# A fused GLA / SSD / Conformer / DeltaNet backbone with MoE on one core: the conformer tiles of the last input projection come one period earlier, and one modulation step comes one group of weights earlier

## The chip, the cores and the metric

One core of a Trainium2 chip runs the whole two-layer model as one program. The metric is the device time of one execution in microseconds, lower is better. The kernel before took 2444.59 us, the median of three runs (2441.27 to 2473.6).

## The reference, cut to what matters

The second layer's mixer (`mixer_cd`) starts with one large input projection and cuts its result into eight kinds of columns:

```python
def cd_stream(h, w_in, b_in, gdn_conv_w, gdn_a_log, gdn_dt_bias):
    bsz, t, _ = h.shape
    ga, gb, q, k, v, og, a_raw, b_raw = split_cols(h @ w_in + b_in, CD_SPLITS)
    glu = ga * jax.nn.sigmoid(gb)
    qkv = jax.nn.silu(dwconv(jnp.concatenate([q, k, v], axis=-1), gdn_conv_w)).astype(F32)
    q, k, v = split_cols(qkv, (GDN_QK, GDN_QK, GDN_V))
    ...
    q = l2norm(heads(q)) * GDN_DK ** -0.5
    k = l2norm(heads(k))

def conformer_conv(u, rows, dw_w, dw_b, ln_g, ln_b):
    bsz, t, ch = u.shape
    y = dwconv(u.reshape(bsz * rows, t // rows, ch), dw_w, dw_b).reshape(bsz, t, ch)
    return jax.nn.silu(layernorm(y, ln_g, ln_b))
```

`glu` has 1024 channels, 8 tiles of 128; its depthwise convolution `conformer_conv` is 31 wide. `q`, `k` and `v` have 8 tiles each too and pass a depthwise convolution that is 3 wide. Context tokens (256) and latent tokens (256) lie side by side, T = 512 columns; the conformer, `q` and the output gate `og` are wanted for the 256 latent tokens alone. The delta-rule scan (`gdn_scan`) follows.

## The kernel before, in words

Activations lie with channels on the 128 partitions and the 512 tokens along the free axis, float32 throughout. The weights stream from HBM through a ring of three slots of 4 MB (`Ring`, `weight_groups`): a group of eight 128-column weight tiles of the projection fills a slot, and so does each half of a modulation step (a slice of the conditioning matmul, loaded by four DMAs of 1 MB). SyncE issues all these loads in the order of `weight_groups`; the load of group n waits until TensorE has used group n - 3, which is counted by the semaphore `w_used`.

The place of the change is the projection of the second layer, `project(PLAN["cd"], ...)`. The list `CD_ALL` names its 49 tiles in the order in which they are computed: first `small` (gates), then eight periods of six tiles: `gb`, `ga`, `k`, `v`, `og`, `q` of one channel chunk. Each engine walks the same list with a loop over j, each in its own program order, and they meet at semaphores:

- TensorE (L489) multiplies tile j: 16 records in the trace for eight k-steps, 512 columns wide for `small`, `k` and `v` (called wide below) and 256 for the others (narrow). It may run four tiles ahead of their copy out of PSUM (`proj_evacuated`). Two tiles behind (`lag=2`), after the matmuls of tile j, it transposes the finished `k`, `v` or `q` tile j - 2 (L504) once `turn_ready` says that it is there.
- ScalarE copies tile j out of PSUM (L1191 for the tiles with a convolution, L1198 for `gb` with a sigmoid and for `ga`, L1208 for `og`). After tile j it finishes the convolution of tile j - 1 with a Silu (L1176), for which it waits for `conv_done`; and it squares the transposed `k` or `q` tile j - 4 for the l2 norm (`kq_squares`, L1169, into `mrow` as scratch).
- VectorE does at step j, in this order: the product `ga * sigmoid(gb)` into `gluR` (L1629) if tile j is a `ga`; the 3-wide convolution (L1650, L1652, L1654) if tile j is `k`, `v` or `q`; the copy of the transposed tile j - 2 (L1658); then some of the 31 taps of the conformer convolution (`conformer_taps`, L1618 for the first, L1620 for the others) by the table `glu_at`; then the steps of `gate_softplus` that are fixed to numbers j (L1675 and L1677 at j = 2, `softplus_head` at j = 8, and so on).

`CONF_STEPS` cuts the 31 taps of a chunk into five portions (7, 6, 6, 6, 6), given out at the step of its `ga` tile and the four after it. So before the change each portion stands alone in its step, and the last one stands in step 48, the last tile's.

Between the tiles come two modulation steps. `CD_MODS = {3: 1, 4: 2}` puts step 1 ahead of the group of tiles number 3 (j = 24) and step 2 ahead of group 4 (j = 32): TensorE multiplies it (L416), ScalarE copies it into `mrow` (L1124), TensorE transposes it from there (L432) one tile later. The same table sets the order of the weight stream in `weight_groups`.

After the tiles `gdn_gates` transposes the gates (L641, L642) as soon as the last `q` tile has been copied; ScalarE takes the root of the squares (L1249) once its last `kq_squares` is done; then the scan starts.

Of the kernel before, what the change touches and what calls it, by code (L numbers as in the profile page):

```python
# [43 lines left out]
AB_GLA = [("small", 0)] + [("q", i) for i in range(4)] + [("k", i) for i in range(4)] \  # L44
    + [("v", i) for i in range(8)] + [("r", i) for i in range(8)]
AB_SSD = [("xs", i) for i in range(8)] + [("bm", 0), ("bm", 1), ("cm", 0), ("cm", 1)] + [("z", i) for i in range(8)]
CD_ALL = [("small", 0)] + [(k, i) for i in range(8) for k in ("gb", "ga", "k", "v", "og", "q")]
CONF_STEPS = [(0, 7), (7, 13), (13, 19), (19, 25), (25, 31)]


CD_MODS = {3: 1, 4: 2}


def weight_groups():


    def mod(layer, r):
        return [(f"mod{layer}{r}", i, 4) for i in range(2)]
# [9 lines left out]
    for i in range(7):  # L68
        if i in CD_MODS:
            g += mod(1, CD_MODS[i])  # L70
        g += [("cd", 8 * i, 1)]
# [25 lines left out]
def hybrid_backbone(nc, A, out):  # L97
    rg = Ring()
    with ExitStack() as ctx:
# [3 lines left out]
        def sb(name, shape, dt=F32, stack=ctx):  # L103
            return stack.enter_context(nc.sbuf_tensor(name, shape, dt))
# [20 lines left out]
        small = sb("small", [P, T])  # L125
# [81 lines left out]
        with ExitStack() as st:  # L207
            gluR = sb("gluR", [P, KD, ROWS, PADW], F32, st)
            og = sb("og", [P, KD, SEQ], F32, st)
# [107 lines left out]
        def plan(stage, tiles, kinds, bias, bias0):  # L317


            made = []  # L320
            for j, (kind, i) in enumerate(tiles):
                how, turn, both = kinds[kind]
                made.append(dict(group=rg.at[stage, j - j % 8], place=j % 8, kind=kind, i=i, how=how,
                                 no=counts["tile"], last=j % 8 == 7 or j == len(tiles) - 1,
                                 turn=counts["turn"] if turn else None, conv=counts["conv"] if how == "conv" else None,
                                 c0=0 if both else SEQ, bias=col(bias, bias0 + j)))
                counts["tile"] += 1
                counts["turn"] += turn
                counts["conv"] += how == "conv"
            return made  # L330

        PLAN = {"gla": plan("gla", AB_GLA, GLA_KINDS, "ab_b", 0), "ssd": plan("ssd", AB_SSD, SSD_KINDS, "ab_b", len(AB_GLA)),
                "cd": plan("cd", CD_ALL, CD_KINDS, "cd_b", 0)}

# [63 lines left out]
        def _(pe):  # L398
# [5 lines left out]
            def modulation_rows(layer, r):  # L404

                first = rg.first[f"mod{layer}{r}"]
                if layer == 0 and r == 0:
                    pe.wait_ge(sg("cond_ready"), 1)
                else:
                    pe.wait_ge(sg("mod_row_copied"), 3 * layer + r)  # L410
                for kh in range(2):
                    group_in(first + kh)
                    w = slot(first + kh).rearrange("p g (k n) -> p g k n", k=4)
                    for k in range(4):
                        for g in range(4):
                            last = mm(ps[6][32 * g:32 * g + 32, :], act_c[:, 4 * kh + k, :], w[:, g, k, :],  # L416
                                      start=(kh == 0 and k == 0), stop=(kh == 1 and k == 3),
                                      tile_position=(0, 32 * g))
                    last.then_inc(w_used, 1)
                pe.drain().then_inc(sg("mod_rows"), 1)  # L420

            def modulation_turn(layer, r):

                pe.wait_ge(sg("mod_row_copied"), 3 * layer + r + 1)
                if layer == 0 and r == 0:
                    pe.wait_ge(sg("norm_ms"), 1)
                else:
                    pe.wait_ge(sg("mod_added"), 3 * layer + r)
                    if r == 0:
                        pe.wait_ge(sg("norm_ms"), 2)  # L430
                for q in range(4):
                    nc.tensor.transpose(ps[7][:, q * P:(q + 1) * P], mrow[:, q * P:(q + 1) * P], ident[:, :])  # L432
                pe.drain().then_inc(sg("mod_turned"), 1)
# [5 lines left out]
            def modulation_between(j):  # L439

                if j % 8 == 0 and j // 8 in CD_MODS:
                    modulation_rows(1, CD_MODS[j // 8])
                if j % 8 == 1 and j // 8 in CD_MODS:
                    modulation_turn(1, CD_MODS[j // 8])

# [1120 lines left out]
        def _(dve):  # L1566
# [46 lines left out]
            def project(made, dest, taps=None, gates=False, between=None):  # L1613
                def conformer_taps(i, lo, hi):
                    y = conf[:, i, :].rearrange("p (r c) -> p r c", r=ROWS)
                    for w in range(lo, hi):
                        if w == 0:
                            V.tensor_scalar(y, gluR[:, i, :, 0:GW], col("conf_w", i), col("conf_b", i), ALU.mult, ALU.add)  # L1618
                        else:
                            V.scalar_tensor_tensor(y, gluR[:, i, :, w:w + GW], col("conf_w", 8 * w + i), y, ALU.mult, ALU.add)  # L1620
                        dve.drain()

                glu_at = {j + n: (p["i"], lo, hi) for j, p in enumerate(made) if p["how"] == "glu" for n, (lo, hi) in enumerate(CONF_STEPS)}
                for j in range(len(made) + 2):
                    if j < len(made) and made[j]["how"] == "glu":

                        i = made[j]["i"]
                        dve.wait_ge(sg("glu_in"), i + 1)
                        V.tensor_tensor(gluR[:, i, :, CK // 2:CK // 2 + GW], gsig[i % 2].rearrange("p (r c) -> p r c", r=ROWS),  # L1629
                                        gval[i % 2].rearrange("p (r c) -> p r c", r=ROWS), ALU.mult)  # L1630
                        dve.drain().then_inc(sg("glu_done"), 1)
                    if j < len(made) and made[j]["how"] == "conv":

                        p = made[j]
                        c, s0 = p["conv"], p["c0"] // SEQ
                        if p["kind"] == "k" and p["i"] == 0 and p["group"] >= rg.first["cd"]:
                            dve.wait_ge(sg("conv_silu"), c)
                            dve.drain()
                            V.memset(cpad2[:, :, :, 0:1], 0.0)
                            V.memset(cpad2[:, :, :, SEQ + 1:SEQ + 2], 0.0)  # L1640
                            dve.drain().then_inc(sg("conv_pads"), 1)
                        dve.wait_ge(sg("conv_in"), c + 1)
                        if c >= 2:
                            dve.wait_ge(sg("conv_silu"), c - 1)
                            before = conv_turn[c - 2]
                            if before is not None:
                                dve.wait_ge(sg("turn_done"), before + 1)
                        to = conv_sum(p)[:, p["c0"]:T].rearrange("p (s t) -> p s t", t=SEQ)
                        w, pad = taps(p), conv_pad(p)
                        V.tensor_scalar(to, pad[:, s0:2, 1:SEQ + 1], w[1], None, ALU.mult)  # L1650
                        dve.drain()
                        V.scalar_tensor_tensor(to, pad[:, s0:2, 0:SEQ], w[0], to, ALU.mult, ALU.add)  # L1652
                        dve.drain()
                        V.scalar_tensor_tensor(to, pad[:, s0:2, 2:SEQ + 2], w[2], to, ALU.mult, ALU.add).then_inc(sg("conv_done"), 1)  # L1654
                    if j >= 2 and made[j - 2]["turn"] is not None:
                        p = made[j - 2]
                        dve.wait_ge(sg("turn_done"), p["turn"] + 1)
                        V.tensor_copy(dest(p), ps[4 + p["turn"] % 2][:, p["c0"]:T].rearrange("p (t c) -> p t c", c=P)).then_inc(sg("turn_copied"), 1)  # L1658
                    if gates and 1 <= j < 24 and j % 3 == 1:
                        gla_magnitude(j // 3)  # L1660
                    if gates and j >= 3 and j % 3 == 0:
                        gla_sums(j // 3 - 1)
                    if j in glu_at:
                        conformer_taps(*glu_at[j])
                    if between is not None:
                        between(j)

# [777 lines left out]
def pack_columns(np, a):  # L2445
# [37 lines left out]
    at0 = COL_AT["cd_b"]  # L2483
    tiles(b, CD_ALL, CD_PLACE)
    for dst, src, n in CD_SMALL:
# [45 lines left out]
def lay_out(np, a):  # L2531
    w2p = np.zeros((P, 8, P), np.float32)
    for d in range(2):
# [6 lines left out]
        "ab_wo": pack_out(np, a["ab_w_out"][0]),  # L2540
        "cd_w": pack_projection(np, a["cd_w_in"][0], CD_ALL, CD_PLACE, CD_SMALL),
        "cd_wo": pack_out(np, a["cd_w_out"][0]),
# [22 lines left out]
```

## Time and profile before

| | |
|---|---|
| median of three runs | 2444.59 us (2441.27 to 2473.6) |
| profiled execution | 2442.07 us, of which its span 2440.3 us |
| TensorE matmul busy | 1991.5 us, 82% |
| VectorE busy | 781.5 us, 32% |
| ScalarE busy | 498.4 us, 20% |
| GpSimd busy | 192.2 us, 8% |
| granted TensorE clock, mean | 0.924 of full speed |
| read from HBM | 524.26 MB, 215 GB/s over the span |

The span is the time from the first to the last instruction of the profiled execution; the execution's own time has 1.8 us more around it. The projection that the change touches runs from 1328 us to 1612 us of the span. In it VectorE is much busier than its 32% over the whole span.

### The profile page before, as it was taken

How to read it: one execution, taken by the hardware profiler on the slowest of the kernel's cores; microseconds unless marked ns; L12 is line 12 of the kernel's file. 1: busy time of each engine (PE TensorE's matmuls, PEld its weight loads, DVE VectorE, ACT ScalarE, POOL GpSimd, SP SyncE). 2: the span in 40 equal slices, each digit the busy share in tenths (PEclk: the TensorE clock that was granted, in tenths of full speed). 3: DMA queues.
4: the chain of work that ended last, by engine and by line, in shares of the span. 5: the costliest groups of instructions: out<-in, count | busy, mean ns of one | idle time of the engine just before them, and what ended most of it. 6: DMA issues, size and time to landing. Idle time of an engine off the chain costs nothing.

```text
span 2440.3 us, 30684 instructions
## 1 busy us (share of the span) xinstructions
PE 1991.5 (82%) x12598; PEld 1040.8 (43%) x12598; DVE 781.5 (32%) x1456; ACT 498.4 (20%) x1037; POOL 192.2 (8%) x230
## 2 busy tenths in 40 slices
PE   5998869987699698898887998979998866666665
PEld 2443744434444333333323655657777622212112
DVE  1112643347710300000002874757765210000001
ACT  2333312222200201000003422344443100000001
POOL 0000000032100000000002100025541000000000
PEclk9999989998999899999999999989998977788887
DMA  9013012250001599999997146110001369999996
GB/s 371 31 69 127 11 58 92 90 208 1 1 35 69 216 416 431 429 433 429 429 430 302 70 157 265 70 70 2 2 2 70 139 274 430 430 431 433 430 431 256
DMA packets 57519, 527.15 MB, mean 216 GB/s; under 512 B 2864, under 2 KB 4144, under 8 KB 43056
## 3 DMA queue, kind: packets, MB, share of 16 engines
q1 hardware_dynamic: 55776, 522.55, 51.5%
q10 hardware_dynamic: 1616, 2.76, 0.3%
q8 instruction: 97, 1.59, 0.3%
q14 instruction: 30, 0.25, 0.0%
HBM read 524.26 MB, written 1.05 MB: 215 GB/s over the span
## 4 chain that ended last, share of the span: by engine, by line
PE 50%; DMA 31%; DVE 9%; issue 3%; ACT 3%; DVEq 1%; PEld 1%; SPq 1%; PEldq 1%; ACTq 0%; POOL 0%
DMA ring<-in_moe_w 28%; PE bank L489 20%; PE bank L988 9%; PE bank L916 5%; PE bank L882 2%; DVE ring L1763 2%; PE bank L594 2%; PE bank L663 1%; PE bank L686 1%; DMA ring<-in_cd_w 1%; DMA router<-in_router 1%; DVE x L2187 1%; DMA ring<-in_ab_w 1%; SPq L296 1%; PEld bank L489 1%
## 5 line engine op out<-in xcount | busy, mean ns | idle before, releaser
L489 PE MATMUL bank<-hT,ring 128*128 128x512 f32 (+1 forms) x1504 | 556.8, 528 | 23.5 <-DMA ring<-in_cd_w 11.2
L988 PE MATMUL bank<-ring,xgs 128*32 128x512 f32 x3072 | 397.0, 672 | 142.7 <-DMA ring<-in_moe_w 141.3
L489 PEld LDWEIGHTS bank<-hT,ring 128*128 128x128 f32 x1504 | 287.4, 194 | 273.2 <-issue 241.6
L988 PEld LDWEIGHTS bank<-ring,xgs 128*32 128x32 f32 x3072 | 111.2, 121 | 401.8 <-issue 309.4
L988 PE MATMUL bank<-ring,hT 128*32 128x512 f32 x1536 | 201.6, 680 | 85.3 <-DMA ring<-in_moe_w 85.3
L2009 DVE SCALAR_TENSOR_TENSOR x<-bank,modT,x 128x256 f32<-128x256 f32 x96 | 42.4, 481 | 480.6 <-PE bank L1014 480.6
L988 PEld LDWEIGHTS bank<-ring,hT 128*32 128x32 f32 x1536 | 56.6, 122 | 217.7 <-issue 165.0
L1998 DVE TENSOR_TENSOR hT<-sils,bank 128x512 f32<-128x512 f32 x24 | 15.8, 686 | 368.5 <-PE bank L988 368.5
L1620 DVE SCALAR_TENSOR_TENSOR x<-gluR,cols,x 128x256 f32<-128x256 f32 x240 | 116.1, 484 | 16.0 <-issue 0.4
L1403 ACT ACTIVATE sils<-bank 128x512 f32<-128x512 f32 x24 | 13.5, 595 | 417.9 <-PE bank L988 417.9
L916 PE MATMUL bank<-mixA,ring 128*128 128x512 f32 x128 | 58.5, 612 | 7.7 <-DVEq L2146 7.7
L594 PE MATMUL bank<-xs_t,x 128*128 (+1 forms) x256 | 38.9, 311 | 28.9 <-DVE x L2124 28.9
L977 PEld LDWEIGHTS bank<-pick,htok 128*128 128x128 f32 x384 | 47.7, 203 | 22.2 <-issue 17.2
L2383 POOL TENSOR_TENSOR ring<-ring,pmask 128x512 f32<-128x512 f32 x40 | 50.9, 1271 | 77.2 <-DVE ring L1751 66.6
L1393 ACT ACTIVATE xgs<-bank 128x512 f32<-128x512 f32 x24 | 14.3, 597 | 206.8 <-PE bank L977 206.8
L916 PE MATMUL bank<-zmix,ring 128*128 128x512 f32 x128 | 56.2, 592 | 0.0
L2367 POOL MEMSET gluR<- 128x3008 f32 x1 | 2.6, 2609 | 679.5 <-DVEq L2019 679.5
L977 PE MATMUL bank<-pick,htok 128*128 128x128 f32 x384 | 52.0, 293 | 4.7 <-DVEq L1980 4.7
L416 PE MATMUL bank<-ring,act_c 128*32 128x512 f32 x384 | 45.6, 628 | 7.8 <-DMA ring<-in_mod_w 6.0
L1419 ACT ACTIVATE pgate<-bank 128x512 f32<-128x512 f32 x24 | 13.5, 595 | 187.4 <-PE bank L988 187.4
L594 PEld LDWEIGHTS bank<-xs_t,x 128*128 128x128 f32 x256 | 35.3, 217 | 38.3 <-issue 29.6
L1014 PE MATMUL bank<-gateT,pgate 128*128 128x256 f32 x192 | 50.6, 394 | 0.3
(451 smaller groups left out, 2385.2 us busy)
## 6 DMA issues: line engine op xcount, KB each, us to landing
ring<-in_moe_w SPq DMA_DIRECT2D x96, 4096.0 KB, 22.4
ring<-in_mod_w SPq DMA_DIRECT2D x48, 1024.0 KB, 11.7
ring<-in_cd_w SPq DMA_DIRECT2D x6, 4096.0 KB, 21.1
ring<-in_ab_w SPq DMA_DIRECT2D x5, 4096.0 KB, 21.7
ring<-in_ab_wo SPq DMA_DIRECT2D x2, 4096.0 KB, 15.5
ring<-in_cd_wo SPq DMA_DIRECT2D x2, 4096.0 KB, 13.6
x<-in_xT SPq DMA_DIRECT2D x1, 2048.0 KB, 10.4
ring<-in_ab_w SPq DMA_DIRECT2D x1, 2048.0 KB, 15.7
```

Of the source, the lines that this page charges most:

```text
L416: last = mm(ps[6][32 * g:32 * g + 32, :], act_c[:, 4 * kh + k, :], w[:, g, k, :], start=(kh == 0 and k == 0), stop=(kh == 1 and k == 3), t ...
L489: last = mm(ps[p["no"] % 4][:, p["c0"]:T], w[:, k, :], hT[:, k, p["c0"]:T], start=(k == 0), stop=(k == KD - 1))
L594: last = mm(ps[2 + hp][:, P * t:P * t + P], mat[hp][:, t * P:(t + 1) * P], tile(t), start=True, stop=True, skip_group_check=True)
L882: last = mm(ps[c % 4][:, SEQ:T], w[:, k, :], conf[:, k, :] if k < 8 else og[:, k - 8, :], start=(k == 0), stop=(k == 15))
L916: last = mm(ps[c % 4][:, c0:T], w[:, k, :], mixed(k), start=(k == 0), stop=(k == 15))
L977: last = mm(ps[(4, 7)[b % 2]][:, k * P:(k + 1) * P], htok[:, 2 * s + tt, ch:ch + P], pick[:, s, tt, P * q:P * q + P], start=(tt == 0), sto ...
L988: last = mm(ps[banks + s][32 * j:32 * j + 32, :], lhs[s][:, 4 * kh + k, 32 * j:32 * j + 32], w[:, j, k, :], start=(kh == 0 and k == 0), st ...
L1014: last = mm(ps[(4, 7)[dt % 2]][:, 256 * s:256 * s + 256], yex[s][:, dt * P:(dt + 1) * P], gateT[:, s, q, :], start=True, stop=True, skip_g ...
L1620: V.scalar_tensor_tensor(y, gluR[:, i, :, w:w + GW], col("conf_w", 8 * w + i), y, ALU.mult, ALU.add)
L1763: last = V.copy_predicated(to[r, :, :, :], mask[r, 0, :].unsqueeze(1).unsqueeze(1).broadcast_to([64, 2, NT, 64]), S)
L2009: last = V.scalar_tensor_tensor(x[:, dt, cc], ps[(4, 7)[dt % 2]][:, cc], mod(layer, 5, dt, s), x[:, dt, cc], ALU.mult, ALU.add)
L2383: G.tensor_tensor(Hb[(l + 1) % 3], Fb[p % 2], pmask[:, l - 1, :].unsqueeze(1).unsqueeze(1).broadcast_to([P, 2, NT, 64]), ALU.mult).then_in ...
```

## The change

`CD_ALL` is written in another order: the `gb` and `ga` tiles of chunk i + 1 stand ahead of the `k`, `v`, `og`, `q` tiles of chunk i. So the list begins `small`, `gb` 0, `ga` 0, `gb` 1, `ga` 1, `k` 0, ..., and the last period has `k`, `v`, `og`, `q` of chunk 7 alone. Since two `ga` tiles now stand two steps apart at the start, `glu_at` holds a list for each step, and two portions of taps can stand in one step. `CD_MODS` puts modulation step 1 ahead of tile group 2 (j = 16) instead of group 3. No tile, tap or byte is added or removed. In the kernel after, the lines behind the edits stand 2 or 6 lines further down.

```diff
-CD_ALL = [("small", 0)] + [(k, i) for i in range(8) for k in ("gb", "ga", "k", "v", "og", "q")]
+CD_ALL = [("small", 0), ("gb", 0), ("ga", 0)]
+for _i in range(8):
+    CD_ALL += [(k, _i + 1) for k in ("gb", "ga") if _i < 7] + [(k, _i) for k in ("k", "v", "og", "q")]
...
-CD_MODS = {3: 1, 4: 2}
+CD_MODS = {2: 1, 4: 2}
...
-                glu_at = {j + n: (p["i"], lo, hi) for j, p in enumerate(made) if p["how"] == "glu" for n, (lo, hi) in enumerate(CONF_STEPS)}
+                glu_at = {}
+                for j, p in enumerate(made):
+                    if p["how"] == "glu":
+                        for n, (lo, hi) in enumerate(CONF_STEPS):
+                            glu_at.setdefault(j + n, []).append((p["i"], lo, hi))
...
-                    if j in glu_at:
-                        conformer_taps(*glu_at[j])
+                    for steps in glu_at.get(j, []):
+                        conformer_taps(*steps)
```

VectorE at the start of the projection, before: the product of chunk 0, seven taps, two gate operations, two memsets, the convolution of `k` 0 (into `wk`), six taps, the convolution of `v` 0, six taps, the copy of the transposed `k` 0.

```order
447 L1629 TENSOR_TENSOR gluR<-rstd,rst64 128x4x64
448 L1618 TENSOR_SCALAR x<-gluR,cols 128x256
449 L1620 SCALAR_TENSOR_TENSOR x<-gluR,cols,x 128x256 x6
450 L1675 TENSOR_SCALAR k_t<-small,cols 64x512
451 L1677 SCALAR_TENSOR_TENSOR v_t<-k_t 64x512
...
457 L1620 SCALAR_TENSOR_TENSOR x<-gluR,cols,x 128x256 x6
458 L1650 TENSOR_SCALAR wk<-wk,cols 128x512
459 L1652 SCALAR_TENSOR_TENSOR wk<-wk,cols 128x512
460 L1654 SCALAR_TENSOR_TENSOR wk<-wk,cols 128x512
461 L1620 SCALAR_TENSOR_TENSOR x<-gluR,cols,x 128x256 x6
462 L1658 COPY k_t<-bank4 128x512
```

The same place after the change.

```order
452 L1622 SCALAR_TENSOR_TENSOR x<-gluR,cols,x 128x256 x6
453 L1635 TENSOR_TENSOR gluR<-rstd,rst64 128x4x64
454 L1622 SCALAR_TENSOR_TENSOR x<-gluR,cols,x 128x256 x6
455 L1620 TENSOR_SCALAR x<-gluR,cols 128x256
456 L1622 SCALAR_TENSOR_TENSOR x<-gluR,cols,x 128x256 x6
...
462 L1622 SCALAR_TENSOR_TENSOR x<-gluR,cols,x 128x256 x12
463 L1656 TENSOR_SCALAR wk<-wk,cols 128x512
464 L1658 SCALAR_TENSOR_TENSOR wk<-wk,cols 128x512
465 L1660 SCALAR_TENSOR_TENSOR wk<-wk,cols 128x512
466 L1622 SCALAR_TENSOR_TENSOR x<-gluR,cols,x 128x256 x12
467 L1664 COPY k_t<-bank4 128x512
```

Between the product of chunk 0 and the copy of `k` 0 there stand now a second product and 50 taps instead of 19. The steps 4 to 6 hold two portions each, and 26 taps (7, 6, 6 and 7) stand ahead of the first convolution instead of 7.

VectorE at the end of the projection, before: the last convolutions (`v` 7, then `q` 7) and copies, each with six taps behind it. The last row is the first of `gdn_gates`.

```order
605 L1650 TENSOR_SCALAR wk<-wk,cols 128x512
606 L1652 SCALAR_TENSOR_TENSOR wk<-wk,cols 128x512
607 L1654 SCALAR_TENSOR_TENSOR wk<-wk,cols 128x512
608 L1620 SCALAR_TENSOR_TENSOR x<-gluR,cols,x 128x256 x6
609 L1658 COPY k_t<-bank5 128x512
610 L1620 SCALAR_TENSOR_TENSOR x<-gluR,cols,x 128x256 x6
611 L1650 TENSOR_SCALAR wk<-wk,cols 128x256
...
614 L1658 COPY v_t<-bank4 128x512
615 L1620 SCALAR_TENSOR_TENSOR x<-gluR,cols,x 128x256 x6
616 L1658 COPY q_t<-bank5 128x256
617 L1700 TENSOR_SCALAR rkq<-rkq 128x48
```

The same place after the change.

```order
605 L1656 TENSOR_SCALAR wk<-wk,cols 128x512
606 L1658 SCALAR_TENSOR_TENSOR wk<-wk,cols 128x512
607 L1660 SCALAR_TENSOR_TENSOR wk<-wk,cols 128x512
608 L1664 COPY q_t<-bank4 128x256
609 L1664 COPY k_t<-bank5 128x512
610 L1656 TENSOR_SCALAR wk<-wk,cols 128x256
611 L1658 SCALAR_TENSOR_TENSOR wk<-wk,cols 128x256
612 L1660 SCALAR_TENSOR_TENSOR wk<-wk,cols 128x256
613 L1664 COPY v_t<-bank4 128x512
614 L1664 COPY q_t<-bank5 128x256
615 L1706 TENSOR_SCALAR rkq<-rkq 128x48
```

The taps are gone from the last steps; the last portion stands four steps earlier.

## Rows read from the trace of the kernel before

**Rows 1.** The page's chain of waits, shares of the span by engine.

```profile
PE 50%; DMA 31%; DVE 9%; issue 3%; ACT 3%; DVEq 1%; PEld 1%; SPq 1%; PEldq 1%; ACTq 0%; POOL 0%
```

**Rows 2.** Waits of PE, 1320 to 1620 us: total us, times, longest.

```profile
PE bank L489 <- DMA ring<-in_cd_w: 11.2, 2, 6.1
...
PE bank L504 <- ACTq L1178: 4.0, 3, 3.6
PE bank L641 <- DVE q_t L1658: 3.2, 1, 3.2
```

**Rows 3.** Groups by line, 1328 to 1614 us.

```profile
L1620 DVE SCALAR_TENSOR_TENSOR x<-gluR,cols,x 128x256 f32<-128x256 f32 x240 | 116.1, 484 | 16.0 <-issue 0.4
```

**Rows 4.** Timeline of PE: start us, us, line, operation, count.

```profile
1328.16 33.69 PE L489 MATMUL bank<-hT,ring 128*128 128x512 f32 x96 [6.88 <-ACT hT L1144]
...
1366.02 3.62 PE L489 MATMUL bank<-hT,ring 128*128 128x256 f32 x16
1369.90 3.69 PE L489 MATMUL bank<-hT,ring 128*128 128x256 f32 x16 [0.26 <-issue]
...
1402.29 7.03 PE L489 MATMUL bank<-hT,ring 128*128 128x512 f32 x16
...
1450.04 7.07 PE L416 MATMUL bank<-ring,act_c 128*32 128x512 f32 x64
1462.22 5.72 PE L489 MATMUL bank<-hT,ring 128*128 128x256 f32 x16 [5.11 <-DMA ring<-in_cd_w]
...
1515.07 6.59 PE L489 MATMUL bank<-hT,ring 128*128 128x256 f32 x16 [6.06 <-DMA ring<-in_cd_w]
...
1606.45 0.69 PE L504 MATMUL bank<-ident,wk 128*128 128x128 f32 x2 [3.58 <-ACTq L1178]
1610.34 1.09 PE L641 MATMUL bank<-ident,small 128*128 128x128 f32 x4 [3.20 <-DVE q_t L1658]
```

**Rows 5.** Timeline of DVE, the first steps of the projection.

```profile
1345.32 0.45 DVE L1629 TENSOR_TENSOR gluR<-rstd,rst 128x256 f32<-128x256 f32 x1 [13.65 <-ACTq L1201]
1345.89 0.44 DVE L1618 TENSOR_SCALAR x<-gluR,cols 128x256 f32<-128x256 f32 x1
...
1349.82 0.48 DVE L1675 TENSOR_SCALAR k_t<-small,cols 64x512 f32<-64x512 f32 x1
...
1351.19 0.06 DVE L1639 MEMSET wk<- 128x4 f32 x1
...
1359.20 0.49 DVE L1650 TENSOR_SCALAR wk<-wk,cols 128x512 f32<-128x512 f32 x1 [1.53 <-ACTq L1193]
...
1361.26 3.28 DVE L1620 SCALAR_TENSOR_TENSOR x<-gluR,cols,x 128x256 f32<-128x256 f32 x6
1364.60 0.69 DVE L1658 COPY k_t<-bank 128x512 f32<-128x512 f32 x1
1365.21 3.28 DVE L1620 SCALAR_TENSOR_TENSOR x<-gluR,cols,x 128x256 f32<-128x256 f32 x6
```

**Rows 6.** Timeline of DVE, the last steps of the projection.

```profile
1604.44 0.35 DVE L1650 TENSOR_SCALAR wk<-wk,cols 128x256 f32<-128x256 f32 x1 [0.17 <-issue]
...
1606.43 3.27 DVE L1620 SCALAR_TENSOR_TENSOR x<-gluR,cols,x 128x256 f32<-128x256 f32 x6
1609.77 0.42 DVE L1658 COPY q_t<-bank 128x256 f32<-128x256 f32 x1
```

**Rows 7.** Timeline of ACT, the last steps of the projection.

```profile
1602.02 0.47 ACT L1191 ACTIVATE wk<-bank,cols 128x256 f32<-128x256 f32 x1 [3.35 <-PE bank L489]
1605.94 0.42 ACT L1176 ACTIVATE wk<-wk 128x256 f32<-128x256 f32 x1 [3.45 <-DVE wk L1654]
1606.53 0.31 ACT L1169 ACTIVATE mrow<-k_t 128x128 f32<-128x128 f32 x1 [0.17 <-DVE v_t L1658]
...
1611.06 1.28 ACT L1249 ACT_TABLE_LOAD   x1
```

**Rows 8.** Timeline of SP, the load that the first wait is for.

```profile
1449.29 0.37 SPq L302 DMA_DIRECT2D ring<-in_cd_w  x1
```

**Rows 9.** Stretches: PE busy (x), then other engines, PEclk, DMA share, GB/s.

```profile
1462.20:1468.00 5.80, 5.78 (x19) 4.75 (x20) 0.00 (x0) 0.02 (x1) 0.00 (x0) 0.65 1.05 388
...
1606.00:1610.00 4.00, 0.69 (x2) 0.29 (x2) 3.55 (x8) 1.64 (x9) 0.00 (x0) 0.53 0.85 352
```

## The prediction

> **What bounds the kernel now.** I read the page's chain first: over the whole span TensorE holds half of it and the waits for weights almost a third [rows 1]. The change touches neither the experts nor any byte, so only the projection's 284 us matter. There TensorE's own waits come next [rows 2]: 11.2 us in two waits for projection weights, 4.0 us for ScalarE ahead of transposes (3.6 of it once) and 3.2 us for VectorE ahead of the gates. All else is TensorE at work: the tiles follow each other without a gap, a narrow one every 3.5 us and a wide one every 6.9 us [rows 4]. So the stage is bound by TensorE, with the two loads after the modulation steps and the tail as the holes.
>
> The tail's hole has VectorE in it. It holds 240 taps of 0.484 us, 116.1 us in all, in this stage [rows 3]. At the end ScalarE has copied `q` 7 out of PSUM at 1602.49, but the convolution begins only at 1604.44, behind six taps; its transposed tile is copied at 1609.77, behind six taps more that began at 1606.43 [rows 6, 7]. TensorE idles 3.58 and 3.20 us there [rows 4]. These taps leave the tail, and that is what the change gives. What it takes is at the other end, where VectorE gets two chunks' taps at once.
>
> **What goes: the tail.** I replay ScalarE's path to its root table load, which stood at 1611.06 [rows 7]. TensorE's last matmul ends at the same time if nothing else moved. Copy at 1602.02, done 1602.49; VectorE is free and starts the convolution some 0.15 later, at 1602.65. From its first operation to the Silu it took 1.50 us (1604.44 to 1605.94), so Silu at 1604.15, done by 1604.57. The transposes began 0.51 after the Silu's start, so at 1604.66; with 0.69 for them the copy starts at about 1605.4, and is visible to ScalarE 0.45 later, at 1605.85. But ScalarE has a task there that was hidden before: the four squares of `k` 7 (0.3 us each), which ran at 1606.53 while VectorE was busy with taps. They now run from 1604.6 to 1605.9, just beside the transposes and the copy. Then come the squares of `q` 7, and the table load at about 1606.8: from the copy's start to the load it was 1.29 us (1609.77 to 1611.06), of which the last 0.8 are these squares. Gain: 1611.06 - 1606.8 = 4.2 us. If the `k` squares fell wholly behind the copy it would be 3 us, and if the clock in the gates' matmuls (0.53 of full speed in 1606 to 1610 [rows 9]) stays up as well, 5 us. I take 4.2.
>
> **What comes: the start.** VectorE's prices are [rows 5]: product 0.57 (1345.32 to 1345.89), first portion of seven taps 3.93 (1345.89 to 1349.82), gate operations 1.37 (1349.82 to 1351.19), wide convolution 2.06 (1359.20 to 1361.26), six taps 3.34 (1361.26 to 1364.60), copy 0.61 (1364.60 to 1365.21); a narrow convolution 1.4 [rows 6]. Walking the new order from the same 1345.32: taps end 1349.8, gates 1351.2, six taps 1354.5, product of chunk 1 1355.1, six taps 1358.45, seven taps 1362.4, the two memsets and `k` 0's convolution 1364.6, two portions 1371.3, `v` 0's convolution 1373.35, two portions 1380.0, copy of `k` 0 1380.6, a portion 1384.0, `q` 0's convolution 1385.4.
>
> TensorE, from the same start: its first group of 96 records ends with `og` 0 at 1361.85 [rows 4]; with two narrow tiles more ahead of it that is 1368.8. Transposes of `k` 0 (0.45), then `q` 0 to 1372.7. Now it wants `v` 0, whose Silu and hand-over follow the convolution by 0.75: 1374.1, a wait of 1.4. Transposes, two narrow tiles, 1381.5. Now it wants `q` 0: 1385.4 plus 0.05 to the Silu and 0.51 from it to the transposes, 1386.0, a wait of 4.5. Together 5.9 us where before there was none. A backlog cannot be larger than the second chunk's work (0.57 + 3.93 + 4 x 3.34 = 17.9) less the 6.9 us of the two tiles that moved ahead and less VectorE's idle time in those steps, 1.53 us of it in the rows shown: 9.5 us. From below it is nothing, if the tiles in front of ScalarE's copies give more room than I count. I take 5.9.
>
> After that VectorE is not late again: a period holds 0.57 + 3.93 + 4 x 3.34 + 2 x 2.06 + 1.4 + 3 x 0.5, some 25 us, against TensorE's 2 x 6.9 + 4 x 3.5 + 1, some 29. The rest of the backlog goes in the first weight wait, and this one comes some 40 us earlier, at j = 16; by the same replay VectorE has nothing to do for 9 us there.
>
> **The clock.** A stop of TensorE costs more than itself. After the idle 5.11 us ahead of 1462.22 the narrow tile took 5.72 instead of 3.6, with 0.65 of full speed granted in 1462.2 to 1468.0; after 6.06 us one took 6.59 [rows 4, 9]. These are stretches at 1.2 GHz between ones at 2.4. The new stop of 4.5 us is the nearest to the first, which cost 2.1 us; nothing shows that 4.5 is enough, so the bounds are 0 and 3.0. I take 2.0.
>
> The Trainium skill ("TensorE: Matmul & The Clock Gate", section "Why this matters for your kernels") speaks against this change: an idle gap between bursts of matmuls sends the engine back to its lower clock. The trace agrees at the two weight waits. By the page's "What's actually happening" the point of switching varies from run to run; the sum would then be 4.0 with the loss and 2.0 without it.
>
> **The two weight waits and the modulation step.** Each wait is for the group of projection weights behind a modulation step. Its load can go out only when the group before it has been used (1449.29 [rows 8]), lands 12.9 us later, and 7.07 us of modulation rows lie beside it [rows 4]. In the stream of the changed kernel the two halves of step 1 stand between tile groups 1 and 2; with three slots the load of group 2 takes the slot of group 1, so it goes out when the tiles of group 1 are done, just ahead of the modulation rows, and the wait is as long as before. The number of DMAs and their bytes are the same; SyncE issues a modulation half in place of tile group 2 before the stage begins, and its rows are wanted only after 16 tiles. Behind the first awaited load now stands another projection load instead of four modulation ones, as behind the second before. That one's wait and first tile together were 12.65 against 10.83; about 0.5 of the difference is that no transposes lie inside that wait, the rest a first tile at a lower clock. Now the places are swapped, so I take +0.3 for both waits together, bounds 0 and 1.1. Moving step 1 costs nothing else: its DVE and ACT parts (two short operations) go where the old ones stood in the period. Left at j = 24 it would copy its row into `mrow` just where ScalarE squares `q` 2 into it, so the order needs the new place.
>
> **Sum.** +5.9 + 2.0 - 4.2 + 0.3 = +4.0 us. On the profiled execution's own 2442.07 that is 2446.1; the median of the runs, 2444.59, lies 2.5 above that execution, and gives 2448.6. I predict 2447. A measurement of this kernel can tell about 2% from no change, 49 us, and nothing in the stage is that large: all TensorE waits in it are 25 us.
>
> **Rivals.**
> - The start's stop is absorbed. If the two stops only eat into the first weight wait, 4.2 us are left as gain: 2438 on the profiled execution. For it: the wait follows 25 us later, and VectorE's backlog does end there. Against: the load goes out when TensorE has used the tiles before it, so it moves with TensorE [rows 8]. Only a load already on its way could absorb anything. Chance 0.15, 2438 to 2443.
> - The backlog spreads. The place is the second period: the portions of chunk 1 and `softplus_head` stand one behind the other ahead of `k` 1 and `v` 1. If each of VectorE's steps is 5% dearer than in my rows (GpSimd is at its masks until 1357), 50 us of backlog make 2.5 us more at `q` 0, and `v` 1 and `q` 1 are late by 1 to 3 us each too, with a second drop of the clock (2 to 3 us). Price: 4.0 + 2.5 + 3 + 2.5 = +12, 2454 on the profiled execution; it decides from where VectorE reaches `q` 0 after about 1388. For it: my replay leaves only tenths between VectorE and TensorE at `v` 1. Against: the period's slack of 4 us. Chance 0.2, 2450 to 2458.
> - The tail's gain isn't real, since ScalarE's table loads or squares set it: +7 instead of +4, 2449. Chance 0.1.
>
> **How the numbers follow.** My forecast, slightly slower and not to be told from no change, has 0.55. The four cases lie between 2438 and 2458, which is the range; it leaves out a median lifted by executions like the one of 2473.6. Faster by over 2%: 0.01. Slower by over 2%: 0.01, for such a draw. Within: 0.98.
>
> **What would show it.** In the timeline of the changed kernel, PE should idle about 1.4 us ahead of the transposes of `v` 0 and 4.5 us ahead of those of `q` 0, near 1373 and 1382 us, released by ScalarE's hand-over, with VectorE's taps without a gap before it. The granted clock there tells the second term: the tiles behind, `k` 1 and `v` 1, take 6.9 us each if it stays up. The waits for projection weights should be two again, near 1420 and 1515, of 5 to 6 us each. The two waits at the tail should fall from 3.58 and 3.20 to about 2 and 0.5, and the root's table load should come 5 us after ScalarE's last copy out of PSUM instead of 9. Wrong would be: a weight wait shortened by the stop before it (first rival), stops at `v` 1 or `q` 1 of over 1 us (second), or a table load that still follows 8 us or more behind the copy (third).

## The result and the profile after

The changed kernel is slightly slower: 2443.86 us (median of 20 runs, 2440.54 to 2449.1) against 2441.15 us for the kernel before in 20 runs. The ratio is 1.0016, with a 95% interval of 1.0009 to 1.0023; that is 3.9 us of 2441 (2.2 to 5.6), well within 2%. The two medians differ by 2.7 us. The prediction was 2447 us, and +4.0 us by its sum.

The span of the profiled execution is 2439.7 us against 2440.3, which looks like a gain and is none: in that execution TensorE reached the projection 5.2 us earlier, through stages that the change does not touch. So I compare a stretch, here and below: from TensorE's first projection matmul to the table load for the root of the squares, the last thing that the change moves. Before it was 1611.06 - 1328.16 = 282.9 us [rows 4, 7]; after it is 1610.19 - 1322.95 = 287.2 us, 4.3 more. What follows that table load is the same, 829.2 us before and 829.5 after. In the profiled executions below it lies between 829.1 and 829.7, except 828.2 in tail_out, while the start of the stretch lies anywhere from 1323 to 1331 us.

TensorE's timeline after, the rows that answer to [rows 4]. Columns are start us, duration us, engine, line and operation; in brackets the idle time ahead and what ended it (a q behind an engine's name, as in ACTq, stands for that engine's sequencer):

```profile
1322.95 40.49 PE L491 MATMUL bank<-hT,ring 128*128 128x512 f32 x128 [6.88 <-ACT hT L1146]
...
1369.75 0.66 PE L506 MATMUL bank<-ident,wk 128*128 128x128 f32 x4 [1.96 <-ACTq L1180]
1370.25 7.07 PE L491 MATMUL bank<-hT,ring 128*128 128x256 f32 x32
1381.68 0.44 PE L506 MATMUL bank<-ident,wk 128*128 128x128 f32 x2 [4.36 <-ACTq L1180]
1381.96 19.05 PE L491 MATMUL bank<-hT,ring 128*128 128x512 f32 x48
...
1421.82 6.14 PE L491 MATMUL bank<-hT,ring 128*128 128x256 f32 x16 [5.69 <-DMA ring<-in_cd_w]
...
1518.17 5.76 PE L491 MATMUL bank<-hT,ring 128*128 128x256 f32 x16 [6.35 <-DMA ring<-in_cd_w]
...
1532.53 0.44 PE L506 MATMUL bank<-ident,wk 128*128 128x128 f32 x2 [0.48 <-ACTq L1180]
1532.81 17.35 PE L491 MATMUL bank<-hT,ring 128*128 128x512 f32 x48
...
1607.98 0.44 PE L506 MATMUL bank<-ident,wk 128*128 128x128 f32 x2 [1.70 <-ACTq L1180]
1609.02 0.63 PE L643 MATMUL bank<-ident,small 128*128 128x128 f32 x4 [0.61 <-DVE q_t L1664]
```

The transposes with four records at 1369.75 are those of `v` 0: TensorE stands still 1.96 us for them. Behind this stop the clock stays up: 32 narrow records take 7.07 us, as elsewhere. Those of `q` 0 (two records) are 4.36 us late. The 48 records behind them, `k` 1, `v` 1 and `og` 1, take 19.05 us, where the same 48 later take 17.35: the clock is at its lower level for a part of them, and that costs 1.7 us. Then the two weight waits, as before, and at the end 1.70 and 0.61 us where there were 3.58 and 3.20.

VectorE's timeline after at the start, answering to [rows 5]:

```profile
1353.57 3.28 DVE L1622 SCALAR_TENSOR_TENSOR x<-gluR,cols,x 128x256 f32<-128x256 f32 x6
1357.03 0.06 DVE L1645 MEMSET wk<- 128x4 f32 x1 [0.18 <-issue]
1357.06 0.06 DVE L1646 MEMSET wk<- 128x4 f32 x1
1358.03 0.49 DVE L1656 TENSOR_SCALAR wk<-wk,cols 128x512 f32<-128x512 f32 x1 [0.90 <-ACTq L1195]
...
1360.08 6.63 DVE L1622 SCALAR_TENSOR_TENSOR x<-gluR,cols,x 128x256 f32<-128x256 f32 x12
...
1368.92 6.63 DVE L1622 SCALAR_TENSOR_TENSOR x<-gluR,cols,x 128x256 f32<-128x256 f32 x12
1375.62 0.69 DVE L1664 COPY k_t<-bank 128x512 f32<-128x512 f32 x1
1376.23 3.27 DVE L1622 SCALAR_TENSOR_TENSOR x<-gluR,cols,x 128x256 f32<-128x256 f32 x6
1379.67 0.35 DVE L1656 TENSOR_SCALAR wk<-wk,cols 128x256 f32<-128x256 f32 x1 [0.17 <-issue]
```

The groups of 12 are the doubled portions. VectorE has one gap of 0.90 us here and otherwise none of 0.2 us or more. It stands ahead of the first convolution, and the prediction did not have it. ScalarE's timeline after shows its other side, and the tail (answering to [rows 7]):

```profile
1357.27 0.69 ACT L1193 ACTIVATE wk<-bank,cols 128x512 f32<-128x512 f32 x1 [10.50 <-DVEq L1647]
...
1605.42 0.47 ACT L1193 ACTIVATE wk<-bank,cols 128x256 f32<-128x256 f32 x1 [3.35 <-PE bank L491]
...
1607.47 0.42 ACT L1178 ACTIVATE wk<-wk 128x256 f32<-128x256 f32 x1 [0.71 <-DVE wk L1660]
...
1610.19 1.28 ACT L1251 ACT_TABLE_LOAD   x1
```

ScalarE may copy `k` 0 into the padded buffer only after VectorE's two memsets of its borders, and these stand in VectorE's program ahead of the first convolution, now behind 26 taps. So ScalarE waits until 1357.27, and VectorE then waits for ScalarE's copy. At the tail the load follows the last copy by 4.77 us instead of 9.04.

### The profile page after: what moved, and what is told of

It is laid out like the page before. It is cut to its first block, busy times and chain, and to the rows that moved or that the text cites. A ratio compares the mean times of both kernels' runs of the same rounds, so it can differ in the third digit from the quotient of the medians.

```text
span 2439.7 us, 30684 instructions
## 1 busy us (share of the span) xinstructions
PE 2001.4 (82%) x12598; PEld 1041.2 (43%) x12598; DVE 781.6 (32%) x1456; ACT 498.1 (20%) x1037; POOL 191.6 (8%) x230
## 4 chain that ended last, share of the span: by engine, by line
PE 49%; DMA 29%; DVE 9%; issue 4%; ACT 3%; PEld 3%; DVEq 1%; SPq 1%; PEldq 1%; ACTq 0%; POOL 0%
DMA ring<-in_moe_w 26%; PE bank L491 17%; PE bank L990 11%; PE bank L918 5%; PE bank L884 2%; PEld bank L491 2%; DVE ring L1769 2%; PE bank L665 2%; PE bank L596 2%; PE bank L688 1%; DMA ring<-in_cd_w 1%; DMA router<-in_router 1%; DVE x L1622 1%; DVE x L2193 1%; PE bank L979 1%
## 5 line engine op out<-in xcount | busy, mean ns | idle before, releaser
L491 PE MATMUL bank<-hT,ring 128*128 128x512 f32 (+1 forms) x1504 | 556.3, 528 | 23.5 <-DMA ring<-in_cd_w 12.0
L990 PE MATMUL bank<-ring,hT 128*32 128x512 f32 x1536 | 208.9, 701 | 76.4 <-DMA ring<-in_moe_w 76.4
L2004 DVE TENSOR_TENSOR hT<-sils,bank 128x512 f32<-128x512 f32 x24 | 15.8, 685 | 373.1 <-PE bank L990 373.1
```

Of the source, the lines that this page charges most:

```text
L491: last = mm(ps[p["no"] % 4][:, p["c0"]:T], w[:, k, :], hT[:, k, p["c0"]:T], start=(k == 0), stop=(k == KD - 1))
L990: last = mm(ps[banks + s][32 * j:32 * j + 32, :], lhs[s][:, 4 * kh + k, 32 * j:32 * j + 32], w[:, j, k, :], start=(kh == 0 and k == 0), st ...
```

## The experiments

Ten more kernels were run beside the kernel before, 5 to 12 executions of each, and one execution of each was profiled. A ratio is of whole executions; a stretch and its stops come from the one profiled execution. "Stretch" is the one defined above; before it is 282.9, after 287.2. A difference of several us between two stretches can be read, one of 1 or 2 us only where its rows are found: the narrow tile behind a weight wait alone took between 5.33 and 6.65 us in these kernels.

| kernel | ratio to before (95%) | stretch us | stops of TensorE at the start us |
|---|---|---|---|
| changed kernel | 1.0016 (1.0009 to 1.0023) | 287.2 | 1.96 and 4.36 |
| order_alone | 1.0017 (1.0008 to 1.0026) | 287.9 | 1.86 and 4.37 |
| mods_alone | 0.9997 (0.9988 to 1.0006) | 280.9 | none |
| no_chunk1 | 0.9984 (0.9975 to 0.9993) | 279.0 | none |
| tail_out | 0.9975 (0.9964 to 0.9986) | 278.3 | none |
| after_own_squares | 1.0024 (1.0015 to 1.0033) | 287.2 | 1.93 and 4.37 |
| spread | 0.9994 (0.9985 to 1.0002) | 279.3 | 0.73, at `k` 1 |
| pads_early | 1.0027 (1.0014 to 1.0039) | 287.0 | 0.83 and 4.37 |
| split | 0.9934 (0.9921 to 0.9947) | 263.4 | none |
| split_double | 0.9941 (0.9924 to 0.9957) | 266.3 | 2.63 |
| split_old_order | 0.9933 (0.9916 to 0.9950) | 264.6 | none |

### The order alone, the modulation step alone, and a control

ScalarE's squares share the buffer `mrow` with the modulation row. For the two halves of the change to be tried apart, the squares of chunks 0 to 4 go to a part of `og` that is not yet in use:

```diff
                     first, v = (0, k_t) if p["kind"] == "k" else (4, q_t)
+                    sq = og[:, 6:8, :].rearrange("p a b -> p (a b)") if p["i"] < 5 else mrow
...
-                        A_(mrow[:, t * P:t * P + P], v[:, p["i"], t, :], ACT.Square, accum_out=rkq[:, p["i"], first + t:first + t + 1])
+                        A_(sq[:, t * P:t * P + P], v[:, p["i"], t, :], ACT.Square, accum_out=rkq[:, p["i"], first + t:first + t + 1])
```

order_alone is the changed kernel with this and

```diff
-CD_MODS = {2: 1, 4: 2}
+CD_MODS = {3: 1, 4: 2}
```

> The new order of the tiles, with modulation step 1 left at j = 24 (ScalarE's squares of chunks 0 to 4 go to another buffer, so that they do not meet the modulation row). Theory (the start costs 6.3 us of stops and 1.7 us of clock, the tail gives 4.3, the place of the modulation step only lets VectorE recover): the start's two stops stay (2.0 and 4.4 us), and since no weight wait follows at 1420, the backlog reaches TensorE once or twice more ahead of q 1 and q 2, 1 to 2 us together; about 6 us slower than before, 2 us slower than the changed kernel. Rival (the slower time comes from the moved modulation step and its loads, not from the order): this kernel is 4 us or more faster than before, by the tail's gain alone.

Measured: 1.0017, a stretch 0.6 us longer than the changed kernel's. The stops at the start are there and the clock drops behind them; the loss belongs to the order. But only one further wait came, 0.33 us. Its place, in TensorE's waits from 1430 to 1460 us of this kernel (us in total, times, longest):

```profile
PE bank L506 <- ACTq L1181: 0.3, 1, 0.3
```

So the theory's second half fell: VectorE does not need the early weight wait. Its slack in a period is enough.

mods_alone is the kernel before with the same buffer and `CD_MODS = {2: 1, 4: 2}`.

> The old order of the tiles, with modulation step 1 at j = 16 (the squares of chunks 0 to 4 in another buffer). Theory: nothing at the start or the tail moves; two weight waits of 5 to 6.5 us as before; within 1 us of before. Rival (the moved step or its loads cost): 4 us or more slower than before, with a longer weight wait near 1420.

Measured: 0.9997, within noise; waits of 5.85 and 6.12 us for the weights. The moved step costs nothing. The stretch is 2.0 us shorter than before, which was not expected: 1.3 us of it is the narrow tile behind the second weight wait, which took 5.33 us instead of 6.59. Whether the moved step gives that back or it is chance, one profiled execution does not show.

after_own_squares is the changed kernel with the buffer alone.

> Control for the two runs with the squares in another buffer: the changed kernel with the squares of chunks 0 to 4 going there. Theory: same instructions, same durations, so the time of the changed kernel within 1 us, 4 us slower than before. Rival (the buffer matters): 2 us or more away from it.

Measured: 1.0024, a stretch of 287.2 us, the same stops. By the medians it is 2.6 us from the changed kernel (2446.46 against 2443.86), by the ratios 2 us, which taken alone is what the rival said; but the two intervals overlap, and by the stretch the difference is nothing. The two profiled executions differ by 8.5 us, 2439.7 and 2448.2 us of span, and all of it lies ahead of the stretch (1322.95 and 1331.42). There TensorE has the same 5882 matmul records and is busy with them for 1132.0 and 1142.0 us, at a mean granted clock of 0.96 and 0.95. So the buffer plays no part in the stages that the change touches, and what separates these two executions is in the stages before.

### Without chunk 1's taps

```diff
-                        for n, (lo, hi) in enumerate(CONF_STEPS):
+                        for n, (lo, hi) in enumerate(CONF_STEPS if p["i"] != 1 else ()):
```

> The changed kernel without the 31 taps of chunk 1 (that part of the convolution is left out). Theory (the backlog of the doubled portions is all of the loss): no stop ahead of the transposes of v 0 and q 0, clock full through k 1 and v 1, the tail as in the changed kernel; 8 us faster than the changed kernel, 4 us faster than before. Rival (the stops come from the wait of ScalarE for the two memsets that now stand behind the taps, or from table loads): the stops stay at 2 us or more, at most 3 us faster than the changed kernel.

Measured: 0.9984, 3.9 us faster than before, and a stretch of 279.0, 8.2 us shorter than the changed kernel's. No stop is left at the start, and the 48 records take 17.35 us. The backlog of doubled portions is the whole of the loss; whether their place or their sum makes it, spread tells below.

### The kernel before without its last taps

```diff
-                glu_at = {j + n: (p["i"], lo, hi) for j, p in enumerate(made) if p["how"] == "glu" for n, (lo, hi) in enumerate(CONF_STEPS)}
+                glu_at = {j + n: (p["i"], lo, hi) for j, p in enumerate(made) if p["how"] == "glu" for n, (lo, hi) in enumerate(CONF_STEPS) if p["i"] < 7 or n < 1}
```

> The kernel before without the last four portions (24 taps) of chunk 7 (left out of the convolution), nothing else changed. Theory (the tail's taps alone hold up the last convolution and copy): from TensorE's last projection matmul to ScalarE's root table load 4.8 us instead of 9.1; 4.3 us faster than before. Rival (another engine sets the tail as well): less than 2 us faster.

ScalarE's last rows in this kernel:

```profile
1604.62 0.47 ACT L1191 ACTIVATE wk<-bank,cols 128x256 f32<-128x256 f32 x1 [3.35 <-PE bank L489]
1606.66 0.42 ACT L1176 ACTIVATE wk<-wk 128x256 f32<-128x256 f32 x1 [1.57 <-DVE wk L1654]
...
1609.38 1.28 ACT L1249 ACT_TABLE_LOAD   x1
```

From copy to load it is 4.76 us instead of 9.04, a gain of 4.3, and the stretch is 4.6 us shorter. The executions gave 0.9975, 6.1 us less (3.4 to 8.8). The tail's gain is real and comes from the taps alone. Of the 6.1 us, 1.0 lies behind the table load (828.2 us instead of 829.2).

### All taps, none doubled

```diff
-                            glu_at.setdefault(j + n, []).append((p["i"], lo, hi))
+                            glu_at.setdefault(j + n + {1: 3, 2: 2, 3: 1}.get(p["i"], 0), []).append((p["i"], lo, hi))
```

> The changed kernel with the portions of chunk 1 three steps later, of chunk 2 two and of chunk 3 one, so that no step holds two portions; all taps are done and the tail keeps its gain. Theory (the cost lies in two portions in one step at the start): the stops ahead of v 0 and q 0 are gone, at most one of 1 us comes at q 1; 7 us faster than the changed kernel, 3 to 4 us faster than before. Rival (VectorE's sum of work, not its place, makes the stop): the stop moves to v 1 or q 1 and stays at 4 us or more, no faster than before.

TensorE in this kernel, at the place where the changed one stops at `q` 0, and on to `k` 1:

```profile
1378.46 0.38 PE L506 MATMUL bank<-ident,wk 128*128 128x128 f32 x2
1378.68 17.35 PE L491 MATMUL bank<-hT,ring 128*128 128x512 f32 x48
...
1400.66 0.66 PE L506 MATMUL bank<-ident,wk 128*128 128x128 f32 x4 [0.73 <-ACTq L1180]
```

The 48 records are back at 17.35 us and one wait of 0.73, for `k` 1, is left. The stretch is 279.3, 8.0 us below the changed kernel's and 3.6 below the kernel before. By the executions it is 0.9994, which cannot be told from before: 1.5 us faster, with 3.5 just inside the interval. Each step gets one portion: the place of the work, not its sum, made the stops.

### The memsets early

```diff
+                    if j == 0 and made[0]["group"] >= rg.first["cd"]:
+                        dve.wait_ge(sg("conv_silu"), made[5]["conv"])
+                        dve.drain()
+                        V.memset(cpad2[:, :, :, 0:1], 0.0)
+                        V.memset(cpad2[:, :, :, SEQ + 1:SEQ + 2], 0.0)
+                        dve.drain().then_inc(sg("conv_pads"), 1)
...
-                        if p["kind"] == "k" and p["i"] == 0 and p["group"] >= rg.first["cd"]:
-                            dve.wait_ge(sg("conv_silu"), c)
...
```

> The changed kernel with the two memsets of the convolution's borders at step 0 of VectorE instead of ahead of k 0's convolution. In the changed kernel ScalarE's copy of k 0 waited 10.5 us behind them, and VectorE then waited 0.9 us for that copy. Theory: VectorE starts k 0's convolution 0.9 us earlier, and each of the two stops is up to 0.9 us shorter, but they follow one behind the other, so that together they lose 0.9 us: about 1 us faster than the changed kernel. Rival (the round trip is hidden behind the backlog): no difference.

TensorE in this kernel:

```profile
1372.69 0.66 PE L506 MATMUL bank<-ident,wk 128*128 128x128 f32 x4 [0.83 <-ACTq L1180]
...
1384.62 0.69 PE L506 MATMUL bank<-ident,wk 128*128 128x128 f32 x2 [4.37 <-ACTq L1180]
1385.10 19.67 PE L491 MATMUL bank<-hT,ring 128*128 128x512 f32 x48
```

The stops lost 1.1 us, all of it in the first, where the theory said 0.9, but the time did not fall: the stretch is 0.2 us shorter and the executions are no faster. After the same stop of 4.37 us the transposes and the 48 records took 0.69 and 19.67 us, against 0.44 and 19.05 in the changed kernel. The clock was down longer. The granted clock in the two kernels (columns: PE, PEld, DVE, ACT and POOL busy with counts, PEclk, DMA share, GB/s), first pads_early, then the changed one:

```profile
1383.00:1400.00 17.00, 15.38 (x32) 7.01 (x33) 15.30 (x26) 2.74 (x11) 0.00 (x0) 0.80 0.00 0
```

```profile
1380.00:1400.00 20.00, 18.32 (x47) 9.25 (x48) 17.58 (x31) 4.86 (x18) 0.00 (x0) 0.91 0.00 0
```

A mean of 0.80 over 17 us is 6.8 us at 1.2 GHz instead of 2.4; a mean of 0.91 over 20 us is 3.6 us, and 3.4 by the records, which took 1.7 us longer than 17.35. In stretches of 1 us the drop also begins at another place: in pads_early TensorE stood still from 1380.25 to 1384.62 and the clock was at 0.50 from 1383 on, while it was still idle; in the changed kernel it stood still from 1377.32 to 1381.68, and the mean was still 1.00 in 1381 to 1382 and 0.69 in the us behind. The longer drop took back 0.9 us of the 1.1 that the shorter stop gave. Each kernel has one profiled execution, so whether pads_early always gets the longer drop is not shown.

### The weight waits, and a version faster than both

The two weight waits are the larger holes of this stage. Here, on top of spread, each modulation step is cut in two halves, and one stands ahead of each of two tile groups, in the stream of loads and in TensorE's program; the rest (the copy, the turn and the addition at the second half) follows:

```diff
-CD_MODS = {2: 1, 4: 2}
+CD_MODS = {1: 1, 4: 2}
...
-        if i in CD_MODS:
-            g += mod(1, CD_MODS[i])
+        for kh in range(2):
+            if i - kh in CD_MODS:
+                g += [(f"mod1{CD_MODS[i - kh]}", kh, 4)]
...
-                if j % 8 == 0 and j // 8 in CD_MODS:
-                    modulation_rows(1, CD_MODS[j // 8])
-                if j % 8 == 1 and j // 8 in CD_MODS:
-                    modulation_turn(1, CD_MODS[j // 8])
+                for kh in range(2):
+                    if j % 8 == 0 and j // 8 - kh in CD_MODS:
+                        modulation_rows(1, CD_MODS[j // 8 - kh], (kh,))
+                if j % 8 == 1 and j // 8 - 1 in CD_MODS:
+                    modulation_turn(1, CD_MODS[j // 8 - 1])
```

> As spread, and in addition each modulation step in two halves, one ahead of each of two tile groups (j = 8 and 16, j = 32 and 40), so that in the stream of loads the halves alternate with the tile groups. Theory (a weight wait is there because the load of the group behind a whole step goes out only when the group before that step is used up): every load goes out a whole tile group ahead, both waits of 6 us and the slow tiles behind them (2 to 3 us each) are gone; 12 to 17 us faster than spread, part of it given back where VectorE has no more waits in which to catch up. Rival (the loads are bound by HBM, not by their start): the waits stay at 3 us or more each and the gain is below 6 us.

TensorE's waits in the projection of this kernel, 1327 to 1591 us (us in total, times, longest):

```profile
PE bank L509 <- ACTq L1183: 2.6, 2, 1.7
...
PE bank L646 <- DVE q_t L1667: 0.6, 1, 0.6
```

No row is left of a wait for `in_cd_w`; of the 2.6 us, 1.7 are at the tail and 0.9 at `q` 3. The stretch is 263.4 us, 15.8 less than spread's: within what was expected. By the executions it is 0.9934, 16.1 us faster than before (12.9 to 19.3). This kind of version is the fastest found, though still under 2%. The bytes are the same, so the moment of issue made the waits. The kernel before shows it too, ahead of the awaited load's issue at 1449.29 [rows 8] and behind it (columns as above, with DMA share and GB/s last):

```profile
1432.00:1449.00 17.00, 17.00 (x49) 8.80 (x47) 14.89 (x37) 4.01 (x15) 0.00 (x0) 1.00 0.01 1
1449.30:1462.20 12.90, 7.63 (x68) 2.40 (x68) 5.93 (x12) 1.54 (x3) 0.00 (x0) 0.89 0.92 354
```

For 17 us the DMA engines have nothing to do, and then they are full until the load has landed.

split_double is split on the changed kernel itself, without the spread.

> As split, but with chunks 1 to 3 as in the changed kernel: two portions of taps in the steps 4 to 6, and no weight wait anywhere. Theory A (the stops at the start cost the same wherever the modulation step stands, and a period's own slack is enough to recover): the stops of 2.0 and 4.4 us are back and a drop of the clock of 1.7 to 3.4 us, 7 to 9 us slower than split in the stretch from the first projection matmul to the root table load, and no more. Theory B (VectorE needs the first weight wait to recover, as the prediction said): further stops of 1 to 3 us each ahead of q 1 and q 2 or later, 11 us or more slower than split.

TensorE, at the start:

```profile
1364.15 3.64 PE L419 MATMUL bank<-ring,act_c 128*32 128x512 f32 x32
...
1381.42 0.44 PE L509 MATMUL bank<-ident,wk 128*128 128x128 f32 x2 [2.63 <-ACTq L1183]
1381.70 19.05 PE L494 MATMUL bank<-hT,ring 128*128 128x512 f32 x48
```

Both theories missed. B fell outright: no further stop of 0.5 us or more until the tail. A had the size wrong: one stop of 2.63 instead of 6.3 in two, 2.9 us more than split over the stretch. The modulation half of 3.64 us now stands at j = 8, just ahead of the tile `q` 0, and gives VectorE that time to catch up; the sizes fit, 6.32 - 3.64 = 2.7, but nothing was run to try it alone. The 1.7 us of clock stayed. These two make 4.3 us; 2.9 are left since split has a stop of 0.89 us at `q` 3 that this kernel has not, and its first 128 records took 40.53 us against 39.99.

split_old_order is the kernel before with split steps, halves at tile groups 2, 3 and 5, 6.

> The old order of the tiles with split modulation steps (halves ahead of the tile groups 2 and 3, and 5 and 6). Theory: gain of the weight waits and of the tail's taps add up, so this is split without the tail's gain: 16 us faster than before in the stretch from the first projection matmul to the root table load (the waits of 5.1 and 6.1 us and the slow tiles of 2.1 and 3.0 us gone), 3.6 us slower than split; the two stops at the tail are 3.6 and 3.2 us, or longer, since the last modulation half now stands ahead of the last tile. Rival (without weight waits VectorE is late throughout, so that the new order's place for the taps matters less or more): a difference to split of 0 or of over 7 us.

Measured: 0.9933 and a stretch of 264.6, 18.3 us shorter than before instead of 16, and 1.1 us longer than split instead of 3.6. That missed both the theory and the rival. Its stops at the tail:

```profile
1588.95 0.44 PE L507 MATMUL bank<-ident,wk 128*128 128x128 f32 x2 [1.32 <-DVE v_t L1661]
1592.80 1.09 PE L644 MATMUL bank<-ident,small 128*128 128x128 f32 x4 [3.41 <-DVE q_t L1661]
```

The stop ahead of the last transposes is 1.32 us and not 3.58, 2.3 us less, near the 2.5 us by which the expectation missed: the last modulation half, ahead of tile 48, gives VectorE 3.6 us for its taps. With the weight waits gone, the order of the conformer tiles moves next to nothing: split, split_double and split_old_order cannot be told apart by their executions.

## Why the prediction was right

Slower by a few us and within 2% was forecast, and that came. Over the stretch, in the terms of the sum:

| term | predicted | measured |
|---|---|---|
| two stops at the start | +5.9 (1.4 and 4.5) | +6.3 (1.96 and 4.36) |
| clock behind them | +2.0 | +1.7 |
| tail | -4.2 | -4.3 |
| weight waits with the tile behind each | +0.3 | +0.5 (23.9 against 23.5) |
| sum | +4.0 | +4.2 by these rows, +4.3 by the stretch, +3.9 by the executions (2.2 to 5.6) |

The mechanism held term by term. That the sum comes within 0.3 us is in part luck: the four misses, +0.4, -0.3, -0.1 and +0.2 us, partly cancel, and the executions alone could not tell 4.0 from 2.5 or 5.5. The absolute forecast of 2447 us came out 3.1 us too high, since it started from a median of three runs, 2444.59, where 20 runs gave 2441.15. Its 25 us of TensorE waits in the stage count 6.9 us that lie ahead of the first tile; inside are 18.4, which changes nothing in the argument.

- **The start.** The walk through VectorE's new order, priced by its old rows, gave the places and nearly the sizes of the stops. The missed piece is the round trip by the two memsets: 0.90 us in which VectorE waits for a copy that ScalarE could not make earlier. pads_early shows that it sits in the first stop (1.96 to 0.83) and not in the second (4.36 and 4.37).
- **The clock.** The stop of 4.4 us lowered it in all four kernels that had it: the 48 records behind took 19.05 us in three and 19.67 in pads_early. Here the Trainium skill's advice against idle gaps ("TensorE: Matmul & The Clock Gate", section "Why this matters for your kernels") and the rows agree. The remark of the Trainium skill that the point of switching varies (the same page, section "What's actually happening") fits pads_early, where the clock fell 2.7 us after TensorE had stopped and in the changed kernel 5.1 us after. The bound of 0 for this term ("nothing shows that 4.5 is enough") was wider than its own rows: a stop of 3.58 us has a clock of 0.53 behind it [rows 4, 9].
- **The tail.** The replay of ScalarE's path held to 0.1 us, with the squares of `k` 7 beside the transposes as written. The 5 us for a clock that stays up did not come: it did stay up (the transposes took 0.44 us instead of 0.69, those of the gates 0.63 instead of 1.09), and the gain was 4.3.
- **The modulation step.** That it costs nothing was right (mods_alone). That the backlog goes "in the first weight wait" was wrong as a need: order_alone, with that wait 40 us later, has one more stop of 0.33 us, and split_double has none.
- **The rivals.** The absorbed stop fell: the first weight wait was 5.69 us, not shorter than the 5.11 before. (It began 34 us behind the stop, not 25.) The spreading backlog fell: no stop above 0.5 us at `v` 1, `q` 1 or later until the tail. The unreal tail fell with tail_out.

## What to carry to other kernels

Moving work of the same amount out of a tail pays only if the place it goes to has room; to see that, walk the engine's new program order with the durations of its old rows and look for the steps that hold two portions. Read a change of a few microseconds from the stretch between its first and last moved instruction: whole executions here differed by 8.5 us at the start of that stretch alone. And a wait for a load in a ring of slots was cured here by letting the load be issued earlier, with large consumers and small ones in turn.

## What the runs showed that was not expected

- A stop of the same length (4.36 and 4.37 us) was followed by 3.4 us of lowered clock in the changed kernel's profile and 6.8 us in pads_early's, so a shorter stop ahead of it need not show in the time.
- A stop of 2.63 us in split_double already lowered the clock (19.05 us for the 48 records), while those of 1.96 and 0.48 us in the changed kernel and 0.73 in spread did not (7.07 us for 32 narrow records behind the first, 17.35 for the 48 behind the second). What decides between 1.96 and 2.63 us was not tried.
- The changed kernel's 20 runs lie in two bunches, 2440.5 to 2442.7 (nine) and 2443.7 to 2449.1 (eleven). Two lengths of the clock's drop behind the stop could make part of that (0.9 us between the profiles), not 5 us. The profiled executions of the changed kernel (2441.45) and of after_own_squares (2449.93) have the same stretch and differ by 8.5 us ahead of it, in TensorE's matmuls at a lower clock. So the bunches come most likely from there; why the clock differs there stays open.
